# Sample attention: keys and values on semaphores of their own, keys loaded as soon as the place's are turned

## The reference, cut to what matters

```python
k_all = jnp.concatenate([hist[0].astype(k_a.dtype), k_a], axis=1)   # 8 x 272 x 8 heads x 64
v_all = jnp.concatenate([hist[1].astype(v_a.dtype), v_a], axis=1)
att = _dsa_block(q_a, q_i, iw, past + jnp.arange(T), k_all, v_all, kidx_all, ...)
# inside, for the selected positions:
logits = jnp.einsum('bqhd,bqkhd->bhqk', q, k_sel) * HEAD_DIM ** -0.5 + bias
probs = jax.nn.softmax(logits, axis=-1)
out = jnp.einsum('bhqk,bqkhd->bqhd', probs, v_sel)
```

## Time and profile before

| | |
|---|---|
| runs | 2340.25, 2342.22, 2330.97 us; median 2340.25 |
| profiled execution | 2339.32 us, of which the span from the first to the last instruction is 2337.5 |
| mean granted clock of TensorE | 0.933 |
| sample_att of layer 0 | 403.65 (last matmul of prompt_att) to 467.70 us (last matmul of the stage) |
| sample_att of layer 1 | 1354.91 to 1418.10 us |
| TensorE busy | 2148.8 us (92% of the span) |

### The profile page before, as it was taken

How to read it: one execution, slowest core, us unless ns; L and a number is a source line. 1 busy time by engine, 2 the same in 40 slices (tenths; PEclk the granted TensorE clock), 3 DMA queues, 4 the chain that set the end, 5 groups by cost and what they waited for, 6 DMA issues and landing times.

```text
span 2337.5 us, 36949 instructions
## 1 busy us (share of the span) xinstructions
PE 2148.8 (92%) x14013; PEld 1849.1 (79%) x14013; DVE 1470.3 (63%) x2156; ACT 1146.3 (49%) x1589; POOL 173.1 (7%) x257
## 2 busy tenths in 40 slices
PE   6999878898999999989998879889999999999996
PEld 4999634598999999989985448778888878888883
DVE  3567544255545454566675425578888888888885
ACT  5421235444434333343212444367777777777773
POOL 3000120110000000000000211100001000000101
PEclk7999679898999999999996889899999999999998
DMA  9222465624545455522231743199999999999995
GB/s 318 60 73 71 135 223 187 226 82 110 163 135 163 135 162 137 160 80 69 73 100 26 239 150 123 58 338 348 367 359 354 356 374 358 380 363 352 347 364 198
DMA packets 285982, 485.87 MB, mean 208 GB/s; under 512 B 21791, under 2 KB 216873, under 8 KB 285857
## 3 DMA queue, kind: packets, MB, share of 16 engines
q1 hardware_dynamic: 265536, 418.72, 52.1%
q0 software_dynamic: 20320, 65.39, 8.0%
HBM read 456.23 MB, written 26.97 MB: 207 GB/s over the span
## 4 chain that ended last, share of the span: by engine, by line
PE 76%; DMA 10%; DVE 6%; ACT 4%; issue 3%; SPq 1%; POOL 1%; ACTq 0%; PEldq 0%; DVEq 0%; PEld 0%; POOLq 0%
PE banks L871 72%; DMA expert_ring<-in_we 5%; PE banks L875 3%; DMA weight_ring<-in_w_ada 2%; ACT region_split L1708 1%; DVE scratch L2295 1%; DVE region L2295 1%; ACT scratch L1708 1%; DVE expert_lower L2295 1%; DMA mix_t<-region 1%; DMA region<-region 1%; SPq L565 1%; DMA scratch<-bias_rows 0%; DVE region_split L2295 0%; ACT hidden_t L1708 0%
## 5 line engine op out<-in xcount | busy, mean ns | idle before, releaser
L2295 DVE TENSOR_TENSOR expert_lower<-expert_ring,region_split 128x1408 fp32r<-128x1408 f32 (+1 forms) x270 | 388.3, 1467 | 27.0 <-ACT region_split L1708 17.3
L871 PE MATMUL banks<-upper_parts,region_split 128*128 128x320 f32 x1664 | 390.7, 310 | 4.5 <-DVE upper_parts L2295 4.5
L871 PE MATMUL banks<-upper_parts,weights_lower 128*128 128x320 f32 (+1 forms) x1248 | 387.2, 310 | 0.0
L871 PE MATMUL banks<-region_split 128*128 128x320 f32 (+1 forms) x1376 | 375.7, 336 | 1.7 <-DVE upper_parts L2295 1.7
L1708 ACT ACTIVATE region_split<-expert_ring 128x1408 fp32r<-128x1408 f32 (+1 forms) x270 | 331.8, 1257 | 61.4 <-DMA expert_ring<-in_we 61.3
L871 PE MATMUL banks<-region_split,upper_parts 128*128 128x512 f32 (+1 forms) x996 | 302.9, 380 | 1.4 <-DVE upper_parts L2295 1.4
L871 PEld LDWEIGHTS banks<-upper_parts,region_split 128*128 128x128 f32 x1664 | 285.1, 189 | 4.8 <-issue 4.8
L871 PE MATMUL banks<-expert_lower,upper_parts 128*128 128x512 f32 x720 | 271.0, 376 | 0.0
L871 PE MATMUL banks<-z_weights_upper,upper_parts 128*128 128x384 f32 (+1 forms) x764 | 238.3, 344 | 24.0 <-DVE region_split L2295 23.9
L871 PEld LDWEIGHTS banks<-region_split 128*128 128x128 f32 x1376 | 244.0, 188 | 18.2 <-DVE upper_parts L2295 1.5
L2295 DVE TENSOR_TENSOR expert_lower<-expert_ring,z_weights_upper 128x1024 fp32r<-128x1024 f32 (+1 forms) x135 | 192.2, 1442 | 73.9 <-ACT z_weights_upper L1708 71.5
(11 more groups left out here) (317 smaller groups left out, 3254.8 us busy)
## 6 DMA issues: line engine op xcount, KB each, us to landing
expert_ring<-in_we SPq DMA_DIRECT2D x240, 704.0 KB, 8.2
expert_ring<-in_we SPq DMA_DIRECT2D x165, 512.0 KB, 4.5
weight_ring<-in_w_ada SPq DMA_DIRECT2D x48, 1024.0 KB, 9.0
weight_ring<-in_w SPq DMA_DIRECT2D x88, 512.0 KB, 4.9
weight_ring<-in_w_in SPq DMA_DIRECT2D x24, 1024.0 KB, 5.3
weight_ring<-in_w SPq DMA_DIRECT2D x16, 1408.0 KB, 6.5
weight_ring<-in_w_out SPq DMA_DIRECT2D x8, 1024.0 KB, 6.5
y_rows<-hidden_t POOLq DMA_DIRECT2D x15, 512.0 KB, 7.5
```

Of the source, the lines that this page charges most:

```text
L871: return nc.tensor.matmul(out, lhsT, rhs, start=first, stop=last)
L2295: return v.tensor_tensor(out, x, y, op)
```

## The change

It splits the loads of a sequence into `load_keys` (on `keys_in[place]`) and `load_values` (values and new values, on `values_in[place]`). For the sequences 4 to 7 POOL loads the keys behind `kv_t_done` alone, and the values behind `pv_done`. These are issued from one loop, in which the keys run three steps ahead of the values. PE waits for `keys_in` (16) in `turn_keys` and for `values_in` (32) ahead of the matmuls on the values. And `take(q_blocks_ready)` goes behind `turn_keys(0)`.

```diff
@@ -731,17 +731,22 @@
-                def load_kv(b):
+                def load_keys(b):
                     place = b % KV_PLACES
-                    load(kv_in[place],
-                         (KVS[place][:, 0, :, :], a["cache_k"][l, b, :, :, :].rearrange("(t p) h d -> p t (h d)", p=P)),
+                    load(keys_in[place],
+                         (KVS[place][:, 0, :, :], a["cache_k"][l, b, :, :, :].rearrange("(t p) h d -> p t (h d)", p=P)))
+
+                def load_values(b):
+                    place = b % KV_PLACES
+                    load(values_in[place],
                          (KVS[place][:, 1, :, :], a["cache_v"][l, b, :, :, :].rearrange("(t p) h d -> p t (h d)", p=P)),
                          (VNW[place][0:TS, :], AV[b * TS:(b + 1) * TS, NTP, :]))
...
                         for b in range(KV_PLACES):
-                            load_kv(b)
+                            load_keys(b)
+                            load_values(b)
...
-                for b in range(KV_PLACES, NB):
-                    pool.wait_ge(kv_t_done, l * NB + b - KV_PLACES + 1)
-                    pool.wait_ge(pv_done, l * (PAIR_UNITS + NB) + PAIR_UNITS + b - KV_PLACES + 1)
-                    load_kv(b)
+                for step in range(NB - KV_PLACES + 3):
+                    if step >= 3:
+                        b = step - 3 + KV_PLACES
+                        pool.wait_ge(pv_done, l * (PAIR_UNITS + NB) + PAIR_UNITS + b - KV_PLACES + 1)
+                        load_values(b)
+                    if step < NB - KV_PLACES:
+                        b = step + KV_PLACES
+                        pool.wait_ge(kv_t_done, l * NB + b - KV_PLACES + 1)
+                        load_keys(b)
...
-                take(q_blocks_ready)
-
                 def turn_keys(u):
-                    take(kv_in[u % KV_PLACES], 48)
+                    take(keys_in[u % KV_PLACES], 16)
...
                 turn_keys(0)
+                take(q_blocks_ready)
                 for u in range(NB + 2):
...
                         wait(*pts[v])
+                        take(values_in[v % KV_PLACES], 32)
```

More of the change, by code:

```diff
@@ L457, in build @@
         q_blocks_ready = sem("q_blocks_ready")
-        kv_in = [sem(f"kv_in{s}") for s in range(4)]
+        keys_in, values_in = [sem(f"keys_in{s}") for s in range(4)], [sem(f"values_in{s}") for s in range(4)]
         kv_t_done, k_t_ready = sem("kv_t_done"), sem("k_t_ready")
```

## The result

| | us |
|---|---|
| the kernel before, 6 runs beside the changed one | median 2336.55 (2330.97 to 2342.22) |
| the changed kernel, 6 runs | median 2316.05 (2307.19 to 2320.44) |
| ratio | 0.9892, 95% interval 0.9865 to 0.9920 |
| the changed kernel, timed again with 9 runs | median 2315.19, ratio 0.9901 (0.9868 to 0.9934) |

The changed kernel is faster by 1.1%. The medians lie 20.5 us apart, and the ratio says 25 us with an interval of 19 to 32. The profiled execution took 2307.19 us (span 2305.2), 32 us less than the profiled execution of before. Only part of that belongs to the change, as the experiments show.

A forecast was written before the change was run, and what follows sets the result against it. TensorE, busy 92%, was taken as the bound, with waits on transfers and query blocks and half clock behind them in two stages. Gains 12.3 + 4.9 + 1.6 = 18.8 us took 2339.3 to 2320.5, range 2312 to 2331.

The forecast's parts named there:

- The sign: Whole kernel: faster, chance 0.78; within 0.5% 0.18; slower 0.04.
- part 1: Steps 3 and 5, both layers: keys no longer wait for the new values; gain 12.3 us, bounds 11.5 to 12.8.
- The clock term: Mask matmul to next first fill, both layers: less time at half clock; gain 1.6 us, 0 to 3.2.
- What bounds the kernel: TensorE, busy 92% of the span; taking its waits from the two stages moves everything behind them.
- Part 1, the reason: Keys of sequence 4: place free long before the load was issued, so issuing early, near 407, removes the wait.
- Rival (a): POOL or the queue holds the early keys, which land with the values as before: 2333 us; chance 0.07.
- Values, weights, new waits: Both stages: values have about 12 us spare, weights arrive in time, 16 new waits cost 0, at most 1.6 us.
- (c): Values become the wait in four sequences per layer: 2328.5 us with an excess of 1 us; chance 0.03.
- (d): Modulation weights come late because early keys share the DMA engines: slower, 2351 us; chance 0.02.
- Part 2, the barrier: Start of both stages: first turning runs beside DVE's query blocks, mask matmul earlier; gain 4.9 us, 4.7 to 5.4.
- The rule on transposes: Start of both stages: transposes don't count as TensorE busy, so the clock gain is 0 and the sum 2322.
- Rival (b): Clock behind the start gives nothing, another half-clock stretch appears in each layer: 2324.7 us; chance 0.13.

The follow-up runs named there:

- four executions of before: The kernel before, unaltered, profiled four times: both stages together took 127.2, 133.6, 126.0 and 130.4 us; the one timed as a change had ratio 0.9998.
- the split alone: The changed kernel with POOL's loads issued at their old place, keys and values still on their own semaphores: median 2312.34 us, ratio 0.9895.
- part 2 alone: The kernel before with only the wait for the query blocks moved behind the first turning: median 2325.05 us, ratio 0.9953.
- part 1 alone: The changed kernel with the wait for the query blocks put back ahead of the first turning: median 2321.52 us, ratio 0.9942.

## Why the prediction was right or wrong, point by point

The sign was right, and so was which waits would go. The forecast was 2320.5; the median, 2316.05, lies inside the range of 2312 to 2331. The gain was forecast too small by every measure: 18.8 us against 20.5 by the medians, 22.3 by the stages and 25 by the ratio. The profiled execution, 2307.19, lies 4.8 us below the range, which I had drawn for a median: 12.7 of its 32 us come from outside the stages, and my 5 us for the spread didn't cover them. The step that failed is the size of part 1, 12.3 us, worked out from one execution. The clock term was mis-sized too, and the reason given for part 1 was wrong.

- **What bounds the kernel** was right: no other engine and no transfer took the place of the waits, and the gain of the stages reached the end of the program.
- **Part 1, the term of 12.3 (11.5 to 12.8).** In the first profile it came to 61.8 - 49.2 = 12.6. Over four executions of before it is 12.6, 19.9, 12.4 and 16.6, a mean of 15.4, outside my bounds. The failed step is that I took the bounds from the undisturbed steps alone (6.05 to 6.38) and treated the disturbed ones (9.77, 9.53, 9.31, 8.36) as known. What a wait costs through the clock was a sample of one: step 3 of layer 0 took 9.8 us in one execution with a wait of 2.3, and 12.3 in another with a wait of 2.6. There step 4 took 9.6 us at the low clock with no wait of its own, and the second wait came in step 6 in place of step 5 (2.65 us, the step 11.2).
- **Part 1, the reason.** I wrote that the place was free for keys long before the load was issued, and took the early issue for what removes the wait. The gain came with the split alone. The trace of before had it. POOL's issue of the keys of sequence 4 stands there:

```profile
423.12 0.72 POOL L674 DMA_DIRECT2D hidden_t<-in_cache_k  x1 [53.02 <-issue]
```

  With 5.5 us to landing these keys are there at 428.6, and the turning was due at about 429.7. I saw that both waits named the new values, and didn't ask whether the keys alone would have been in time. Rival (a) was priced as if late issue meant the old wait, which the split run refutes: late issue gives the full gain. The wrong reason didn't touch the number only because the change splits the semaphores as well; that was luck.
- **Values, weights, new waits.** No wait on a value load and none on a weight chunk, as forecast. Ahead of the matmuls with two semaphores TensorE does stand idle, for 0.96 us in step 2 and up to 0.47 later, but these waits end on ACT's probabilities and stood there before too; behind the turnings of the sequences 4 and 6, where the old transfer waits had hidden them, they are new with 0.20 to 0.36 us. My bound of 0.1 each wasn't needed for the semaphore and didn't see these. Rivals (c) and (d) didn't show.
- **Part 2, the barrier, 4.9 (4.7 to 5.4).** Measured 6.16 - 3.95 = 2.2 and 6.96 - 3.86 = 3.1: 5.3.
- **The clock behind the start, 1.6 (0 to 3.2).** The first profile gave (5.57 - 4.79) + (5.70 - 4.79) = 1.7, but its upper bound was too low: where the clock stays full, step 0 takes 3.39, and both layers together gain 4.5. I had used a step of 3.8 us that contained a turning of modulation rows (0.47 us) that step 0 lacks.
- **The rule on transposes**, by which this term would be 0: the term was 1.7 in one execution and 3.1 in the next, (5.57 - 4.79) + (5.70 - 3.39). The time doesn't decide for or against the rule itself.
- **Rival (b)**, a further stretch of low clock in each layer: in the kernels with split semaphores and four places none of the steps 1 to 6 was at the low clock.

## What to carry to other kernels

A wait on a group of transfers ends with the last of them. Before you move a load, look at which transfer of the group the wait names and whether the consumer reads that one: here a semaphore of its own for each consumer was the whole gain of the loads, and loading earlier paid only with three places in place of four. Price a short idle stretch of TensorE from several executions, because the low clock behind it lasted from about 3 to 17 us here.

## What the runs showed of the hardware

- The length of the low clock behind an idle stretch of 2.3 to 2.6 us was about 3 us in one execution and 17 us in another of the same code, while TensorE was busy nearly throughout. Over the four executions of before and part 2 alone, the clock fell during or just behind all 14 transfer waits of 1.8 to 2.7 us, and the three of 1.0 us. At the other six, of 0.3 to 0.9 us and of 1.35, it stayed full. The low clock lasted about 3 us at 13 of the 17, about 7 at two and 17 at two.
- DVE's eight copies of the query blocks, 1.28 us in the kernels in which POOL issues nothing beside them, took 1.35 to 1.45 us in both layers of those with the early keys, where POOL issues the first keys at the same moment. In part 1 alone POOL issues the first keys 2.7 us behind the last copy, and the copies take 1.28 us again. Compare the changed kernel and then the split alone:

```profile
401.31 1.45 DVE L2302 COPY hidden_t<-region 64x128 f32<-64x128 f32 x8
```

```profile
403.21 1.28 DVE L2298 COPY hidden_t<-region 64x128 f32<-64x128 f32 x8
```

  The first mask matmul waits for these copies. Where the wait stands behind the first turning and DVE's work is unchanged, it stands 3.86 to 3.96 us behind the start with the early keys and 3.78 or 3.79 without them. The early issue costs 0.1 to 0.2 us per layer there, another reason not to want it with four places.
